# Attention masks added on VectorE inside the maximum, and head norms spread by one matrix product a tile

## The reference, cut to what matters

```
def masked_softmax(s, mask):
    s = jnp.where(mask, s.astype(jnp.float32), -jnp.inf)
    m = jnp.max(s, axis=-1, keepdims=True)
    p = jnp.exp(s - m)
    return p / jnp.maximum(jnp.sum(p, axis=-1, keepdims=True), 1e-30)

q = rope(rms_norm(q, g_q), pos, ...)      # one root-mean-square a head and token
s = einsum('qd,kd->qk', q, k) * scale
p = masked_softmax(s, k_pos <= q_pos)     # or a mask of chosen keys
o = einsum('qk,kd->qd', p, v)
```

## Time and profile before

| what | value |
|---|---|
| median of 3 runs | 3644.54 us (3640.66 to 3647.4) |
| the profiled execution's own time | 3644.65 us |
| its span, first to last instruction | 3642.5 us |
| granted TensorE clock, mean | 0.981 of full speed |
| TensorE busy | 3495.4 us, 96% of the span |
| VectorE busy | 2069.7 us, 57% |
| ScalarE busy | 1416.5 us, 39% |
| GpSimd busy | 1683.3 us, 46% |

### The profile page before, as it was taken

The page is one execution under the profiler, slowest core; times in us unless marked ns, Lnnn a source line. Parts: engine busy times, 40 slices in busy tenths (PEclk is TensorE's granted clock), DMA queues, the critical chain, the costliest instruction groups (busy, mean ns, idle before and its releaser), DMA issues. The chain is left out here.

```text
span 3642.5 us, 46587 instructions
## 1 busy us (share of the span) xinstructions
PE 3495.4 (96%) x16468; PEld 2855.3 (78%) x16468; DVE 2069.7 (57%) x3134; ACT 1416.5 (39%) x2480; POOL 1683.3 (46%) x917
## 2 busy tenths in 40 slices
PE   7998999999999999999999999989999999999998
PEld 6876877788878778877887777778877777778877
DVE  5768745212367776561123666648864665648953
ACT  3245652322333456432322446233333446333332
POOL 3346544344434365434443654435543654435543
PEclk9999999999999999999999999989999999999999
DMA  4311023222232110232343220533343221432322
GB/s 163 104 53 35 24 87 110 87 98 93 92 118 99 47 36 24 96 112 89 102 142 119 76 82 24 179 122 109 127 144 117 70 82 37 177 116 104 128 91 92
DMA packets 96755, 346.74 MB, mean 95 GB/s; under 512 B 12624, under 2 KB 13264, under 8 KB 95952
## 3 DMA queue, kind: packets, MB, share of 16 engines
q1 hardware_dynamic: 96592, 344.62, 27.4%
HBM read 338.15 MB, written 6.29 MB: 95 GB/s over the span
## 5 line engine op out<-in xcount | busy, mean ns | idle before, releaser
L226 POOL TENSOR_TENSOR weights_lo<-arena,weights_hi 128x1024 fp32r<-128x1024 f32 x467 | 1195.0, 2559 | 1509.3 <-ACT weights_hi L200 1508.5
L200 ACT ACTIVATE weights_hi<-arena 128x1024 fp32r<-128x1024 f32 x491 | 517.5, 1054 | 627.7 <-PE ps L638 389.7
L294 PE MATMUL ps<-moving_hi,weights_hi 128*128 128x512 f32 x2256 | 567.7, 394 | 11.7 <-ACT weights_hi L200 6.7
L294 PE MATMUL ps<-moving_lo,weights_hi 128*128 128x512 f32 x2256 | 559.6, 390 | 0.0
L294 PE MATMUL ps<-moving_hi,weights_lo 128*128 128x512 f32 x2256 | 558.0, 389 | 0.0
L294 PEld LDWEIGHTS ps<-moving_hi,weights_hi 128*128 128x128 f32 x2256 | 424.0, 189 | 103.2 <-ACT weights_hi L200 7.1
L294 PEld LDWEIGHTS ps<-moving_lo,weights_hi 128*128 128x128 f32 x2256 | 424.4, 189 | 88.1
L294 PEld LDWEIGHTS ps<-moving_hi,weights_lo 128*128 128x128 f32 x2256 | 422.9, 188 | 88.1 <-POOL weights_lo L226 1.2
L1087 POOL TENSOR_SCALAR arena<-arena 128x128 f32<-128x128 f32 (+2 forms) x240 | 225.5, 953 | 212.1 <-DVE arena L992 131.4
L247 DVE TENSOR_TENSOR moving_lo<-arena,moving_hi 128x512 fp32r<-128x512 f32 x196 | 178.4, 961 | 232.4 <-ACT moving_hi L242 232.4
L2215 DVE SCALAR_TENSOR_TENSOR arena<-ps,arena 128x512 f32 x64 | 44.1, 691 | 305.2 <-PE ps L294 292.6
(11 more groups left out here) (372 smaller groups left out, 5541.2 us busy)
## 6 DMA issues: line engine op xcount, KB each, us to landing
arena<-wstream SPq DMA_DIRECT2D x532, 512.0 KB, 3.3
arena<-modw SPq DMA_DIRECT2D x64, 512.0 KB, 3.7
arena<-modw_first SPq DMA_DIRECT2D x32, 512.0 KB, 4.4
layer_input<-arena SPq DMA_DIRECT2D x2, 2048.0 KB, 6.9
arena<-layer_input SPq DMA_DIRECT2D x2, 2048.0 KB, 8.2
arena<-xT SPq DMA_DIRECT2D x4, 512.0 KB, 5.3
outT<-arena SPq DMA_DIRECT2D x8, 256.0 KB, 2.1
arena<-con SPq DMA_DIRECT2D x1, 1413.5 KB, 9.4
```

Source lines behind the costliest of these rows:

```text
L200: m.nc.scalar.activation(m.w_hi[:, j % 2, :], slab(m, base + at), ACT.Copy).then_inc(hi_ready, 1)
L226: m.nc.gpsimd.tensor_tensor(m.w_lo[:, j % 2, :], slab(m, base + (j if at is None else at)), m.w_hi[:, j % 2, :].bitcast(F32), ALU.subtract)\
L294: mm = m.nc.tensor.matmul(bank, unit_tile(w, k), a[:, k, :], start=(p == 0 and k == 0), stop=(p == 2 and k == KD - 1))
```

## The change

Three edits in `attention_stage`: the mask products (line 918) are gone; `rowmax` becomes one two-operand operation which adds the mask from SBUF, negates, writes the result back over the scores in PSUM and gives the minimum; the exponential takes the scale -1. GpSimd first builds a 128x512 float32 tile in SBUF, 384 zero columns and the 128-column triangle, of which each block takes its last columns, and VectorE waits for that once a stage. The selected masks stay the bf16 tiles that they were.

In `head_norm_stage` `row_hi` and `row_lo` become one tile of 101 rows (0 to 36 and 64 to 100, zeros between, cleared by VectorE), and the selection matrices get the same selection twice, so that one product a tile does what two did. ScalarE makes them later: six copies behind the square root, two more (the pairs') behind the high row. The filler passes move to behind the tiles 3, 6, 9 and so on.

```
 # attention_stage, TensorE
-                        bias, c0 = biases(j, b, qt)
-                        for n_, (q, k) in enumerate(terms(j, b)):
-                            nc.tensor.matmul(o, q[:, qt * P:(qt + 1) * P], k[:, 0:w], start=(n_ == 0), stop=False)
-                        mm = nc.tensor.matmul(o[:, c0:w], m.ident_bf, bias, start=False, stop=True)
+                        products = terms(j, b)
+                        for n_, (q, k) in enumerate(products):
+                            mm = nc.tensor.matmul(o, q[:, qt * P:(qt + 1) * P], k[:, 0:w], start=(n_ == 0), stop=(n_ == len(products) - 1))
 # VectorE
-                        r = nc.vector.tensor_reduce(mx[:, 4 * (u % 2) + qt:4 * (u % 2) + qt + 1],
-                                                    m.ps[:, bank, c:c + P * (qt + 1)], AX, ALU.max, negate=True)
+                        s = m.ps[:, bank, c:c + P * (qt + 1)]
+                        r = nc.vector.tensor_tensor_reduce(s, s, masks(u // nb, qt), -1.0, HUGE, ALU.add, ALU.min,
+                                                           mx[:, 4 * (u % 2) + qt:4 * (u % 2) + qt + 1])
...
+            dve.wait_ge(masked, 2)
             rowmax(0)
 # ScalarE
-                                                 ACT.Exp, bias=mx[:, s:s + 1], accum_out=sums[:, s:s + 1])
+                                                 ACT.Exp, bias=mx[:, s:s + 1], scale=-1.0, accum_out=sums[:, s:s + 1])
 # GpSimd
+            nc.gpsimd.memset(causal[:, 0:T - P], 0.0).then_inc(masked, 1)
+            nc.gpsimd.tensor_copy(causal[:, T - P:T], m.causal_bf).then_inc(masked, 1)
 # head_norm_stage, ScalarE
-            nc.scalar.activation(picks, m.ident[0:COLS, 0:COLS], ACT.Copy).then_inc(picked, 1)
...
             nc.scalar.activation(rstd[:, :, 0:ROOTS], var[:, :, 0:ROOTS], ACT.Sqrt).then_inc(rooted, 1)
+            for part, at in halves:
+                count = part.stop - part.start
+                nc.scalar.activation(picks[part, :], m.ident[part, at:at + COLS], ACT.Copy).then_inc(picked, 1)
+                heads = key_picks[part].rearrange("k (h d) -> k h d", d=MQK)
...
             act.wait_ge(turned, 1)
+            act.wait_ge(cleared, 1)
             nc.scalar.activation(row_hi, m.ps[0:COLS, 6, :], ACT.Copy).then_inc(cut_hi, 1)
+            for part, at in halves:
+                nc.scalar.activation(pairs[part].rearrange("k (h d) -> k h d", d=DH), m.ident[part, at + 16:at + 28]
...
             fill.high(act, 1)
 # VectorE
+            nc.vector.memset(row[32:LOW, :].bitcast(F32), 0.0).then_inc(cleared, 1)
 # TensorE
-                nc.tensor.matmul(m.ps[0:r, n % 5, 0:c], pick, row_hi[:, 0:c], start=True, stop=False)
-                nc.tensor.matmul(m.ps[0:r, n % 5, 0:c], pick, row_lo[:, 0:c], start=False, stop=True).then_inc(spread, 1)
-                if n >= 4 and n % 3 == 1:
+                nc.tensor.matmul(m.ps[0:r, n % 5, 0:c], pick, row[:, 0:c], start=True, stop=True).then_inc(spread, 1)
+                if n and n % 3 == 0:
                     fill.product(pe, n // 3 + 2)
```

More of the change, by code:

```diff
@@ L842 @@
 SCORE_BANKS = ((0, ((3, 0),)), (1, ((0, 0), (2, 128))), (2, ((1, 0),)))
+HUGE = 3e38
 PROB_AT = {0: 0, 1: 128, 2: 384, 3: 768}
@@ L871, in stacked_keys, with attention_stage @@
         in_turn(pool, cut, m.nc.gpsimd.tensor_tensor(m.r(low)[n:n + 64, :], rows, m.r(high)[half:half + 64, :].bitcast(F32), ALU.subtract))
-def attention_stage(m, nb, terms, values, biases, weights, out, spread, add=False, gates=(), base=0, taps=None, heads=NH):
+def attention_stage(m, nb, terms, values, masks, causal, weights, out, spread, add=False, gates=(), base=0, taps=None, heads=NH):
     nc = m.nc
@@ L882, in attention_stage @@
     mx, sums, rinv = m.small[:, 0:8], m.small[:, 8:16], m.small[:, 16:24]
[L883 removed]
+    with stage(m, "masked scores maxed exped inverted scaled transposed hi_out lo_out pv_done side_out half_out o_out diag_done tapped "
                   + Beside.NAMES) as (block, (
[L885 removed]
+            masked, scores, maxed, exped, inverted, scaled, transposed, hi_out, lo_out, pv_done, side_out, half_out, o_out, diag_done, tapped, *side_sems)):
         fill = Beside(m, base, gates, 7, side_sems)
@@ L1272, in head_norm_stage @@
     sums, nsa_sums = by_token(taken[:, 0:TT * MLA_SUMS], MLA_SUMS), by_token(taken[:, NSA_SUMS:NSA_SUMS + 48], 12)
-    row_hi, row_lo, picks, pairs, key_picks = (m.r(a)[0:COLS, :] for a in m.spreading)
+    LOW, ROWS = 64, 64 + COLS
+    row, picks, pairs, key_picks = (m.r(a)[0:ROWS, :] for a in m.spreading)
+    row_hi, row_lo = row[0:COLS, :], row[LOW:ROWS, :]
     picks = picks[:, 0:COLS]
+    halves = (slice(0, LOW), 0), (slice(LOW, ROWS), LOW)
     over_heads = lambda a: a.rearrange("p (t o) -> p t o", o=1).to_broadcast([P, TT, 8])
@@ L1280, in head_norm_stage @@
     tiles += [(m.raw[:, 5 + n, :], ("pair", n), None) for n in range(6)] + [(m.kcmp[0:64, :], ("query", 28), None)]
-    with stage(m, "picked sums_out filled varied rooted step inverted sized turned cut_hi cut_lo spread normed "
+    with stage(m, "picked cleared sums_out filled varied rooted step inverted sized turned cut_hi cut_lo spread normed "
                   + Beside.NAMES) as (block, (
-            picked, sums_out, filled, varied, rooted, step, inverted, sized, turned, cut_hi, cut_lo, spread, normed, *side)):
+            picked, cleared, sums_out, filled, varied, rooted, step, inverted, sized, turned, cut_hi, cut_lo, spread, normed, *side)):
         fill = Beside(m, C1["gate"], gates, 5, side)
@@ L1300, in _ @@
             nc.scalar.activation(taken[:, NSA_SUMS:SUMS], m.ps[:, 6, NSA_SUMS:SUMS], ACT.Copy).then_inc(sums_out, 1)
-            nc.scalar.activation(picks, m.ident[0:COLS, 0:COLS], ACT.Copy).then_inc(picked, 1)
-            nc.scalar.activation(pairs.rearrange("k (h d) -> k h d", d=DH), m.ident[0:COLS, 16:28].rearrange("k (h o) -> k h o", o=1)
-                                 .to_broadcast([COLS, 12, DH]), ACT.Copy).then_inc(picked, 1)
-            heads = key_picks.rearrange("k (h d) -> k h d", d=MQK)
-            for rows, first in ((slice(0, MNOPE), 8), (slice(MNOPE, MQK), ROOTS)):
-                nc.scalar.activation(heads[:, :, rows], m.ident[0:COLS, first:first + 8].rearrange("k (h o) -> k h o", o=1)
-                                     .to_broadcast([COLS, 8, rows.stop - rows.start]), ACT.Copy).then_inc(picked, 1)
             fill.high(act, 0)
@@ L2231, in first_layer @@
     head_norm_stage(m, gates[0:3])
-    causal = lambda j, b, qt: (m.causal_bf, qt * P)
+    after = lambda tile: lambda j, qt: tile[:, T - P * (qt + 1):T]
     attention_stage(m, 1, lambda j, b: ((m.q_mla[0:MQK, j, :], m.k_mla[0:MQK, j, :]),), lambda j, b, kt: m.r(m.v_mla)[:, kt, j, :],
-                    causal, lambda j, b: None, lambda pair: m.o_mla[:, pair, :], tile(61), gates=gates[3:5], base=C1["gate"] + 3, taps=TAPS_FRONT)
+                    after(tile(62)), tile(62), lambda j, b: None, lambda pair: m.o_mla[:, pair, :], tile(61), gates=gates[3:5], base=C1["gate"] + 3, taps=TAPS_FRONT)
     compressed_attention_stage(m, gates[5:9], C1["gate"] + 5)
@@ L2239, in first_layer @@
     attention_stage(m, 2, lambda j, b: [(m.r(m.q_cut)[:, j, :], m.r(k)[:, 2 * b + j // 4, :]) for k in (m.k_hi, m.k_lo)],
-                    lambda j, b, kt: m.r(m.v_nsa)[:, kt, 2 * b + j // 4, :], causal,
+                    lambda j, b, kt: m.r(m.v_nsa)[:, kt, 2 * b + j // 4, :], after(tile(9)), tile(9),
                     lambda j, b: branch[:, :, 3 * j + 1 + b], lambda pair: m.o_nsa[:, pair, :], tile(5), add=True,
```

16 lines of the change are left out of this document (10 added, 6 removed).

## The result

The changed kernel takes 3620.59 us (median of 4 runs, 3617.45 to 3622.14) where the kernel before took 3645.82 on the same chip: ratio 0.9932, 95% interval 0.9916 to 0.9947, so 25.2 us or 0.7% faster. The forecast was 3626.9 us in a range from 3608 to 3644: the sign is right and the time lies in the range. The profiled execution has a span of 3619.1 us against 3642.5, and the mean granted clock is 0.980 against 0.981, so the clock as a whole doesn't explain the difference.

The account below looks back on a forecast made before the run. It took VectorE's loop with ScalarE to have almost no room, TensorE pacing the second kind. Per layer pair: MLA +1.8, NSA -1.8, second kind -3.9, head norms -5.0, so -8.9; two pairs -17.8: 3626.9 us, range 3608 to 3644.

Parts of the forecast that it names:

- A: The forecast itself: 0.12 us an operation; VectorE paces MLA, NSA and the selected units; 3626.9 us; chance 0.45.
- B: Second result of the new maximum is free, 0.02 us an operation; TensorE paces NSA and second kind: 3611.6 us; chance 0.19.
- C: Read-out of the new maximum costs 0.18 us, 0.20 an operation, 0.55 a cycle: 3641.5 us; chance 0.18.
- D: Addition with minimum streams at half rate, 1.3 us a cycle; VectorE paces every attention stage: 3689 us; chance 0.13.
- E: Mask products weren't worth 0.40 us; attention pays 0.31 us a cycle, head norm gain stays: 3643 us; chance 0.05.
- The new maximum: VectorE, attention: add with minimum replaces the reduction, 0.02 us more stream and 0.10 for the second result: 0.12 an operation.
- The cycle: VectorE's attention loop: waits for three of four new maxima, less 0.05 us to spare: 0.31 us longer (0.01 to 0.55).
- NSA: NSA attention stage: VectorE's 6.14 us replaces 6.22; 13 cycles give -1.0, two at the start 0.8: -1.8 us.
- Second kind: Second-kind attention stage: selected cycles -0.6, causal cycles 2.8 us gained, about 0.5 at the start: -3.9 us.
- The mask tile: GpSimd's tile at each attention stage's start: hidden, costs nothing; 0.5 us a stage, 3 in all, if cover is missing.
- Head norms: Head norm stage: 23 products go (5.3 us), root 0.7 earlier, 0.7 and 0.3 us given back: -5.0 us.
- Signs named in the forecast: Wrong if: operation above 0.9 or below 0.72 us, first maximum held by GpSimd's tile, filler pass waiting, or new half clock.

Follow-up runs that it names:

- One more maximum: Changed kernel with the mask tile made by VectorE, plus one unused maximum over 256 elements a unit, between third and last maxima: 3613.66 us.
- the product issued twice: Changed kernel with each of the 23 spreading products of a head norm stage issued two times, 101 rows: 3630.49 us.
- masks alone: Kernel before with only the attention masks changed, head norm stage left as it was: 3634.82 us, ratio 0.9974.
- tile by VectorE: Changed kernel, but VectorE instead of GpSimd makes the mask tile: 3606.69 us, ratio 0.9887.
- after run again: The changed kernel itself, unaltered, measured a second time on another chip: 3620.37 us, ratio 0.9923.

## Why the prediction was right, point by point

**The sum** was short by 7.4 us (25.2 against 17.8), with errors of both signs. By its time the case lies between A and B, and the second result is indeed cheap and not free; but that is partly chance, since about 4 of the missing 7.4 us come from the head norms, which every rival had at 5.0 a stage. Rivals C and D also price eight cycles of MLA where A has seven (at seven they give 3640.4 and 3686.6 us), and the -1 a pair of E can't be redone from the paces named; the forecast itself uses none of them.

**The new maximum, 0.12 us an operation.** Right in kind: a read-out that is an instruction of its own, as the forecast had it by the Trainium skill, VectorE: DVE Perf Modes, section on two Vector instructions with no wait between them. The size was three times too large: the four maxima of a unit took 0.16 us more, 0.04 each. By its rows the operation is 9 ns longer for 128x512 and 46 to 52 ns for the shorter forms, and the successor starts 0.61 us behind the start of the 128x512 one. The first maximum reaches ScalarE 0.07 us later.

**The cycle, 3 x 0.12 - 0.05 = 0.31 us: this is the step that failed.** It counted three of four maxima on the path; one is. I had the rows for it: the wait for ScalarE in the earlier trace rows ends at the last exponential's sum, and that chain starts at the first maximum. The argument that ScalarE's second exponential might have to wait was true at the edge and came to 0.04 us. Measured: 0.10. It mis-sized MLA (+1.8 forecast, 0 measured: 0.7 us of cost is balanced by 0.7 us that the products were worth, all of it in the first two cycles, where the forecast had 0.4) and the selected units of the second kind (6.15 forecast, 5.9 measured). And it put rival D's break-even at 0.22 us an operation. One more maximum shows that 0.3 us in front of the last maximum costs nothing.

**NSA, a mean of 6.14 us in place of 6.22: right number, wrong reason.** The last 13 cycles average (89.62 - 3.78 - 6.03) / 13 = 6.14 us. But they alternate between 5.7 us, the same with the new operation and without any mask, and 6.7 to 6.8, which is the loop at 6.57 + 0.10. So the -1.0 for 13 cycles was met. The -0.8 for the start wasn't: in layer 2 the third unit's first maximum starts 12.0 us behind the first score in before and in after. And between the last unit's first maximum and the stage's end 0.7 us is lost in both layers, for which the forecast had nothing. That makes the -0.3 of layer 2; in layer 1 before has more half clock at the start (its first cycle is 5.85 us and in layer 2 4.64), and the stage comes out at -1.4.

**Second kind, -3.9.** -6.2 and -4.6. In layer 1 the seven causal cycles gave 3.2 us (49.0 to 45.8), where the forecast had 2.8, and the six selected ones 2.2 (37.5 to 35.4), where it had 0.6: this term was held back by the 6.15. The end of the stage and the pass behind it gave 0.7 more, which weren't in the sum. The 0.5 for the start wasn't met: the third unit's first maximum starts 12.4 us behind the first score in before and in after in layer 1, where before has a stretch at half clock, and 1.5 us later than before in layer 2, where it has none. That is the mask tile, and the difference between the layers.

**The mask tile, nothing, with 0.5 us a stage if the cover is missing.** Wrong for the second kind, where it is 1.4 us of TensorE's waits and 1.6 us of the stage; right for MLA and NSA, where the first cycle takes the delay. The cost was looked for in the duration of the two operations and not in when GpSimd begins.

**Head norms, -5.0.** -7.0 at equal clock. The product term was 5.3 for 23 products and measures 4.1 in its own right; VectorE, now close behind TensorE, gives part of it back, for which the forecast had 0.7: ahead of the next stage's first product TensorE stands idle for 1.07 us in after, 0.57 with the product issued twice and 0.45 in before. What was missing is 2.6 us for the height of the array. The rows were there: the earlier trace rows is taken from inside a group of products, where a neighbour costs 0.23 us, and the two ends of a group weren't looked at. The earlier root, 0.7, is 0.5 to 1.1, and it isn't ScalarE's queue that held it but GpSimd behind it.

**Signs named in the forecast.** Two signs of being wrong came true, though the kernel was faster than forecast: an operation under 0.72 us (0.69) and a first maximum held up by GpSimd's tile. No filler pass waited behind the pair copies. New waits of TensorE for VectorE's low parts came in NSA (3.0 us in the stretch of layer 1, 0.7 before); in MLA the new waits are for ScalarE's high parts (3.1 us, 0.9 before). The half clock after new gaps isn't shown for MLA: after had it in layer 1 in front of the compressed attention, and so had masks alone and tile by VectorE, while after run again had not, with the same code. In the second kind of layer 2 there is a pattern: all seven profiles with GpSimd's mask tile have a stretch at half clock near the start of the stage, and none of the seven others has. In five of the seven it begins ahead of the tile's wait, so the wait isn't shown to be the cause, and the cause stays open.

## What to carry to other kernels

An engine's "own cycle" that holds a wait for another engine is a loop through both; before an operation in it is priced, follow which of its results the other engine starts from. Work behind that point was free here up to 0.3 of a wait of 0.55 us. When products of unlike height alternate on TensorE, count the changes of height and not only the products, and give the small ones more rows where rows are free: 101 paid nothing here, 37 did. And a stage's small set-up belongs to the engine that is awake when the stage starts.

## What the runs showed of the hardware that I had not expected

- A tensor-tensor operation with a second, reduced result costs on VectorE 690 ns for 128x512 against 681 for the plain reduction (329 against 283 for 128x128), and its read-out (140 ns by its row) overlaps with the next operation: 128x128 starts at the same moment as the read-out in front of it.
- Between 128-row and 37-row products TensorE loses 0.41 us for a change there and back (3.61 against 3.20 us a period); between 128 and 101 rows it loses nothing.
- A VectorE operation on 32 columns took 1.12 us beside GpSimd's low parts and 0.18 us ahead of them. The Trainium skill, SBUF — State Buffer, Who interferes with whom, has the two engines share one pair of ports, which one of them holds for a whole instruction, when VectorE's operation has two SBUF inputs or runs in a two-port mode. The operation of 1.12 us has one input, and no row shows its mode; the one behind it, with two inputs, took 1.21 us against 0.19. The trace agrees, with 0.9 and 1.0 us.
- A short stretch at half clock costs 1.5 to 1.7 us in the head norm stage and nothing where TensorE would have waited for the mask tile anyway, and two profiles of one kernel differ by 7 us in the parts that nobody touched. With effects of some microseconds, the stage of the record says more than the sum.
